# Norm chains in halves at four layer boundaries, and work moved off VectorE in a two-block transformer kernel

## What is computed

```python
def rms_norm(x, g):
    y = x * rsqrt(mean(x * x, axis=-1) + EPS)
    return y * g
for layer in range(2):                      # first block
    a = rms_norm(h, g[layer, 0])
    m = mla_mixer(a) if layer == 0 else hgrn2_mixer(a)
    h = h + rms_norm(m, g[layer, 1])        # post-norm
    a = rms_norm(h, g[layer, 2])
    h = h + rms_norm(relu(a @ w1)**2 @ w2, g[layer, 3])   # post-norm
# second block: rms_norm, dsa_mixer (top-k of indexer scores, then attention), conv FFN,
# rms_norm, retention_mixer, conv FFN
```

## Time and profile before

| | |
|---|---|
| median of 3 runs | 2640.44 us (2637.19 to 2641.26) |
| profiled execution | 2637.47 us, span 2635.7 us |
| PE busy | 2568.2 us, 97% |
| POOL busy | 1938.6 us, 74% |
| DVE busy | 1104.4 us, 42% |
| ACT busy | 662.3 us, 25% |
| HBM traffic | 85 GB/s mean |

### The profile page before, as it was taken

The page is one execution under the profiler, slowest core; times in us unless marked ns, Lnnn a source line. Parts: engine busy times, 40 slices in busy tenths (PEclk is TensorE's granted clock), DMA queues, the critical chain, the costliest instruction groups (busy, mean ns, idle before and its releaser), DMA issues.

```text
span 2635.7 us, 32594 instructions
## 1 busy us (share of the span) xinstructions
PE 2568.2 (97%) x11823; PEld 2089.6 (79%) x11823; DVE 1104.4 (42%) x1907; ACT 662.3 (25%) x1110; POOL 1938.6 (74%) x1664
## 2 busy tenths in 40 slices
PE   6999999998999899999998999999999999999999
PEld 5777888887888688888776888888877877888887
DVE  6543211126767432112587352525442332643433
ACT  2443111014444311001355221203112022321111
POOL 5455988886666588888580888887967856888784
PEclk8999999999999999999998999999999999999999
DMA  5122323332222222332210233332212212333231
GB/s 155 53 72 64 96 96 95 96 97 79 65 77 67 64 96 96 96 95 88 72 65 17 80 96 96 96 98 95 96 64 95 80 64 80 96 96 104 88 108 68
DMA packets 287877, 224.26 MB, mean 85 GB/s; under 512 B 13491, under 2 KB 281756, under 8 KB 287644
## 3 DMA queue, kind: packets, MB, share of 16 engines
q1 hardware_dynamic: 287196, 222.44, 27.5%
q10 hardware_dynamic: 576, 0.40, 0.1%
HBM read 220.72 MB, written 2.10 MB: 85 GB/s over the span
## 4 chain that ended last, share of the span: by engine, by line
PE 90%; DVE 5%; issue 1%; DVEq 1%; ACT 1%; DMA 0%; POOL 0%; ACTq 0%
PE proj L617 26%; PE proj L619 26%; PE proj L618 26%; PE aux L2218 1%; DVE top L1768 1%; DVEq L1771 1%; PE proj L642 1%; PE proj L647 1%; PE proj L643 1%; PE aux L2022 1%; PE aux L2192 1%; PE aux L853 1%; PE proj L795 1%; PE aux L465 0%; PE proj L1961 0%
## 5 line engine op out<-in xcount | busy, mean ns | idle before, releaser
L617 PE MATMUL proj<-a_hi,w_hi 128*128 128x512 f32 x1992 | 795.1, 399 | 0.0
L619 PE MATMUL proj<-a_hi,w_lo 128*128 128x512 f32 x1992 | 776.6, 390 | 0.0
L618 PE MATMUL proj<-a_lo,w_hi 128*128 128x512 f32 x1992 | 775.9, 389 | 0.0
L1245 POOL TENSOR_TENSOR w_hi<-raw,small 128x512 fp32r<-128x512 f32 x373 | 392.9, 1053 | 442.5 <-PE proj L619 343.6
L1252 POOL TENSOR_TENSOR w_hi<-raw,small 128x512 fp32r<-128x512 f32 (+2 forms) x449 | 486.1, 1083 | 187.5 <-PE proj L619 187.3
L1257 POOL TENSOR_TENSOR w_lo<-raw,w_hi 128x512 fp32r<-128x512 f32 (+2 forms) x449 | 592.4, 1319 | 6.0
L1256 POOL TENSOR_TENSOR w_lo<-raw,w_hi 128x512 fp32r<-128x512 f32 x372 | 483.9, 1301 | 29.1
L617 PE MATMUL proj<-g_hi,w_hi 128*128 128x512 f32 x1200 | 470.0, 392 | 0.9 <-POOL w_lo L1257 0.5
L619 PE MATMUL proj<-g_hi,w_lo 128*128 128x512 f32 x1200 | 467.0, 389 | 0.0
L618 PE MATMUL proj<-g_lo,w_hi 128*128 128x512 f32 x1200 | 466.9, 389 | 0.0
L617 PEld LDWEIGHTS proj<-a_hi,w_hi 128*128 128x128 f32 x1992 | 374.5, 188 | 82.8 <-issue 5.3
(11 more groups left out here) (289 smaller groups left out, 2301.9 us busy)
## 6 DMA issues: line engine op xcount, KB each, us to landing
raw<-in_mlp_w SPq DMA_DIRECT2D x64, 1024.0 KB, 5.3
raw<-in_f_w_up SPq DMA_DIRECT2D x88, 512.0 KB, 4.6
raw<-in_b_w_in SPq DMA_DIRECT2D x24, 1024.0 KB, 5.2
raw<-in_hgrn_w_in SPq DMA_DIRECT2D x32, 512.0 KB, 4.9
raw<-in_f_w_down SPq DMA_DIRECT2D x16, 1024.0 KB, 4.9
raw<-in_b_w_out SPq DMA_DIRECT2D x8, 1024.0 KB, 5.1
raw<-in_f_w_down SPq DMA_DIRECT2D x8, 768.0 KB, 4.3
raw<-in_a_w_in SPq DMA_DIRECT2D x5, 1024.0 KB, 5.2
```

Of the source, the lines that this page charges most:

```text
L617: pe.matmul(psum[r][:], w_hi[r][:, w], xh, start=k == 0, stop=False)
L618: pe.matmul(psum[r][:], w_hi[r][:, w], xl, start=False, stop=False)
L619: last = pe.matmul(psum[r][:], w_lo[r][:, w], xh, start=False, stop=k == kc - 1)
L1245: first = pool.tensor_tensor(hi[:, 0:n], src[:, 0:n], nothing.to_broadcast([P, n, P]), ALU.subtract)
```

## The change

Four parts.

1. **Post-norm in two halves of 256 tokens**, at the four boundaries. The sums of the two halves go to two banks, `aux[0]` and `aux[3]`; the last square, the last matmul with ones, Ln, Exp, the multiplication and addition of tile 0 and its `a_hi` are each done per half. ACT's order is Ln 0, Exp 0, Ln 1, Exp 1; the next stage's first matmul still waits for both halves. After an MLP the last `acc` addition is halved too, and the sum of squares of tile 6 comes ahead of it. After an output projection the copy of the last bank goes from ACT to DVE.
2. **Products of ones.** `keep_running` puts matmuls of the ones matrix with itself (128 columns, into an unused bank) into PE's stream: 2 ahead of the half sums (MLPs only), 9 after them (all four).
3. **Start.** The range reduction of the angles, its sines and the sign go behind `take_c(1)`; ACT reloads the logarithm and exponential table after the sines. The tables are loaded one slab later than the small rows.
4. **Selections.** `r_square` and `r_col` are scaled on ACT; the key tile is made by ACT (gain) and POOL (root); both `q_refine` move to POOL, after the splits of query unit 7 and of output unit 2; the indexer's last projection is taken before the key tile is made, and its sum of squares comes before the first score.

```diff
+            def square_half(self, act, src, s):
+                if s == 0:
+                    act.wait_ge(sq_used.sem, self.base + self.chunks - 1 - len(self.tiles))
+                act.activation(self.last[:, HALVES[s]], src[:, HALVES[s]], ACT.Square).then_inc(sq_ready.sem, 1)
...
+                for bank, h in zip(self.banks, HALVES):
+                    last = pe.matmul(bank[:, h], ones[:], self.total[:, h], start=True, stop=False)
+            def sum_half(self, pe, s):
+                h = HALVES[s]
+                pe.wait_ge(sq_ready.sem, self.base + self.chunks + s)
+                pe.matmul(self.banks[s][:, h], ones[:], self.last[:, h], start=False, stop=True).then_inc(sq_used.sem, 1)
+            def root(self, act):
...
+                for s, h in enumerate(HALVES):
+                    act.wait_ge(sq_used.sem, self.base + self.chunks + s)
+                    act.activation(log_ms[:, h], self.banks[s][:, h], ACT.Ln, bias=eps,
+                                   scale=1.0 / self.size).then_inc(logs[s][0], 1)
+                    act.wait_ge(*logs[s])
+                    act.activation(rstd[:, h], log_ms[:, h], ACT.Exp, scale=-0.5).then_inc(roots[s], 1)
...
+        def keep_running(pe, n):
+            for _ in range(n):
+                pe.matmul(aux[2][:, 0:P], ones[:], ones[:], start=True, stop=True)
...
             def dve(self, dve, then=None):
-                dve.wait_ge(*self.norm.ready())
-                for c in range(DC + 1):
+                for s, h in enumerate(HALVES):
+                    scaled, added = (self.scaled, self.added) if s else (self.half_scaled, self.half_added)
+                    dve.wait_ge(*self.norm.half_ready(s))
+                    dve.scalar_tensor_tensor(tmp[0][:, h], tile(acc, 0)[:, h], gain("norm", self.gain_at), rstd[:, h],
+                                             ALU.mult, ALU.mult).then_inc(scaled.sem, 1)
+                    dve.wait_ge(*scaled.at(0))
+                    dve.tensor_tensor(tile(hT, 0)[:, h], tile(hT, 0)[:, h], tmp[0][:, h], ALU.add).then_inc(added.sem, 1)
+                for c in range(1, DC + 1):
...
                 turns_from(pe, self.st.turns, block)
                 self.post.norm.sum(pe)
+                keep_running(pe, 2)
+                for s in range(2):
+                    self.post.norm.sum_half(pe, s)
+                keep_running(pe, 9)
...
+                bank = arrived(act, self.st, DC - 1)
+                for s in range(2):
+                    self.post.norm.square_half(act, bank, s)
...
+                dve.tensor_copy(tile(acc, DC - 1), psum[self.st.bank(DC - 1)][:]).then_inc(*taken(self.st, DC - 1))
...
                         if st.slab_base + q == 2:
-                            small_loads()
+                            row_parts()
+                        if st.slab_base + q == 3:
+                            late_tables()
...
+            def key_scaled():
+                pool.wait_ge(*key_gained.at(0))
+                pool.wait_ge(*n_key.ready())
+                pool.tensor_tensor(dsa_kT, dsa_kT, rstd, ALU.mult).then_inc(key_ready.sem, 1)
...
+                            if st is st_dsa and j == Q0 + 4:
+                                key_scaled()
+                            if st is st_dsa and j == Q0 + DSA_HEADS - 1:
+                                q_refine(0)
+                            if st is st_dsa_o and j == RING - 2:
+                                q_refine(1)
...
-            sine(0, rope_sin, reduced)
-            sine(1, rope_cos, reduced_cos)
             act.wait_ge(norms_ready, 1)
             pre_mla.act(act, h_ready.at, mla_factor)
...
             square_c(1)
+            sine(0, rope_sin, reduced)
+            sine(1, rope_cos, reduced_cos)
+            log_and_exp(act)
...
-            dve.wait_ge(*r_ready.at(2))
-            dve.tensor_scalar(r_square[:], r_square[:], 1.0 / DSA_LAT, None, ALU.mult).then_inc(r_factors.sem, 1)
...
-                    if b == TB - 1 and n == rounds - 2:
-                        q_refine(0)
...
-                if b == 1:
-                    dve.wait_ge(*n_key.ready())
-                    dve.scalar_tensor_tensor(dsa_kT, dsa_cT, qk_gain[:], rstd, ALU.mult, ALU.mult).then_inc(key_ready.sem, 1)
```

More of the change, by code:

```diff
@@ L228, in program @@
         inv_freq, rope_sign, eps = (tab["small"][:, k:k + 1] for k in range(3))
-        zero, halves = tab["small"][:, 3:4], tab["small"][:, 4:6]
+        zero, halves, three = tab["small"][:, 3:4], tab["small"][:, 4:6], tab["small"][:, 6:7]
         lb = sb("lb", 8 * DC)
@@ L493, in ready @@
                 return rstd_ready.sem, i * self.gper + self.gbase + g + 1
+        HALVES = (slice(0, T // 2), slice(T // 2, T))
+        half_log, half_rstd = (shared(f"half_{k}", turns=4) for k in ("log", "rstd"))
         class AddedNorm(Norm):
@@ L531, in program, with __init__ @@
         class LastDirect(AddedNorm):
+            made = 0
+            def __init__(self, chunks, total, load=False):
+                super().__init__(chunks, total, load=load)
+                Norm.squares += 1
+                self.made = LastDirect.made
+                LastDirect.made += 1
+                self.last, self.banks = self.tiles[(chunks - 1) % len(self.tiles)], (self.bank, aux[3])
+            def square_half(self, act, src, s):
+                if s == 0:
+                    act.wait_ge(sq_used.sem, self.base + self.chunks - 1 - len(self.tiles))
+                act.activation(self.last[:, HALVES[s]], src[:, HALVES[s]], ACT.Square).then_inc(sq_ready.sem, 1)
             def add(self, dve, c):
@@ L547, in sum, with half_ready @@
                 pe.wait_ge(sq_used.sem, self.base + self.chunks - 2)
[L548 to L551, removed]
+                for bank, h in zip(self.banks, HALVES):
+                    last = pe.matmul(bank[:, h], ones[:], self.total[:, h], start=True, stop=False)
+                last.then_inc(sq_used.sem, 1)
+            def sum_half(self, pe, s):
[3 more added lines that the diff above has]
+            def root(self, act):
+                if self.gbase > 0:
+                    act.wait_ge(rstd_ready.sem, self.gbase)
+                logs = (half_log.at(self.made), (log_ready.sem, self.gbase + 1))
+                roots = (half_rstd.sem, rstd_ready.sem)
+                for s, h in enumerate(HALVES):
[4 more added lines that the diff above has]
+                    act.activation(rstd[:, h], log_ms[:, h], ACT.Exp, scale=-0.5).then_inc(roots[s], 1)
+            def half_ready(self, s):
+                return self.ready() if s else half_rstd.at(self.made)
         class PairedNorm(Norm):
@@ L918, in act @@
                 turns(act, self.st.turns, block)
-                for c in range(DC):
+                for c in range(DC - 1):
                     emptied(act, self.st, DC + c, self.st.turns - 1)
                     self.post.norm.square(act, tile(acc, c), c)
+                act.wait_ge(*self.half_taken.at(0))
+                self.post.norm.square_half(act, tile(acc, DC - 1), 0)
+                emptied(act, self.st, 2 * DC - 1, self.st.turns - 1)
+                self.post.norm.square_half(act, tile(acc, DC - 1), 1)
                 self.post.norm.root(act)
@@ L978, in pe @@
                 self.post.norm.sum(pe)
+                for s in range(2):
+                    self.post.norm.sum_half(pe, s)
+                keep_running(pe, 9)
             def act(self, act):
-                for m in range(DC):
+                for m in range(DC - 1):
                     bank = arrived(act, self.st, m)
```

122 lines of the change are left out of this document (71 added, 51 removed).

## The result

The changed kernel takes 2624.23 us (median of 5, 2622.59 to 2627.60), the kernel before beside it 2639.40: ratio 0.9947, 95% interval 0.9936 to 0.9957. Its profiled execution is one of 2622.59 with a span of 2620.6, 15.1 shorter than that of before. The forecast of 2625.3 is 1.1 us off. Later runs will show that one of its three terms, the boundaries, came out near its number by chance in this one execution.

What follows compares the result with a forecast made beforehand. PE was taken as the bound, busy 97% of the 2635.7 us span. Start 6.8, boundaries 3.0 and selections 5.3 sum to 15.1 us off 2640.4, giving 2625.3 us; range over the cases 2612 to 2634, the sum's own 2619 to 2631.

Steps and rivals of the forecast that it cites:

- Start, 6.8 us: Kernel start: first matmul at 21.9 instead of 28.76 us, less 0.1 booked against it; gain 6.8 us.
- nearly filled: Between take_c(1) and PE's need of the squares, some 15 us: moved work fills nearly all; 0.1 us booked, 1.5 far bound.
- Boundaries, the arithmetic: Restarts after the four post-norms, from halved chains: 0.1 us later, 0.55 earlier, 0.5 later, 0.5 earlier.
- the alternation with GpSimd: At the boundaries, DVE and POOL operations alternate one for one; a half operation costs a whole POOL operation plus 0.28 us.
- Boundaries, the clock: Four post-norm boundaries: gains of 7.7 us with the clock up, about 0.2 with it down; 3.0 us booked.
- everything fits: Rival: clock stays up at three or four boundaries and DVE slips between POOL's operations; 25 us, 2616; chance 0.20.
- Selections, 5.3 us: Sparse attention: net 3.2 us from DVE's chain, 1.2 and 0.5 between its halves, 0.4 from reordering; sum 5.3 us.
- the meeting with GpSimd: Sparse attention: POOL's later splits slow DVE's normalizations and the selection's last step; 1.6 us lost.
- the reordering: Ahead of the first score: one PE wait goes, another comes, DVE's sum may end earlier; +0.4 us.
- One part gives nothing: Rival: one of start, boundaries or selections yields no gain; 8 us in all, 2632; chance 0.14.

Runs made afterwards that it cites:

- no products: Changed kernel without any products of ones, the post-norm chains still in halves: 2625.78 us.
- the kernel with the boundaries undone: Changed kernel with the four post-norm chains whole again and no products of ones, start and selections kept: 2624.57 us, and 2624.95 when run again.
- more products and GpSimd held: Changed kernel with 12 products (22 at the third boundary) and GpSimd's two w_lo operations held until DVE's last a_lo tile: 2618.23 us, ratio 0.9918.

## Why the prediction came out right, point by point

- *Start, 6.8 us.* Right: first matmul at 21.87 for 21.9, shift 7.7 and 7.5 in the changed kernel, 7.2 in the mean of twelve. What lies above is the clock, which I hadn't counted: from the first matmul to the eighth the shift grows from 6.9 to 7.6. The "nearly filled" 15 us were filled to the last: nothing lost in the changed kernel, 0.64 once the start came 1.4 earlier still.
- *Boundaries, the arithmetic.* Right within 0.1 at all four restarts (no products), and the alternation with GpSimd is shown by holding GpSimd back: 1.37 becomes 0.43. The Trainium skill (SBUF — State Buffer, "Who interferes with whom") has the port pair that the two engines share as an exclusive lock; these rows agree.
- *Boundaries, the clock.* The gains with the clock up were right within 0.2 (1.3, 2.0, 0.9, 2.9). The chances were a third, a half, nothing and a half; in the five traces with nine products the clock was up at boundaries 1 to 4 in four, two, none and four, 2.0 a trace for my 1.3. What failed is that the term had one more step: next in line at the second and fourth boundary is the sum of squares at L533, 1.9 us of the 7.7. And 3.0 us of mean gain (2.7 by its own parts: 0.4, 1.4, -1.0 and 1.9) was booked as if it were certain, while its scatter, and that of the low stretches elsewhere, is as large. In the median the term is 0 +/- 1.5. The reason given for "everything fits" was a reading that misleads: the clock was indeed at 1.00 while PE waited at the shorter stops, but in the same trace it fell at 1300.8 us, 4.4 us behind a stop of 0.45 and with none since. So shorter stops are no safeguard.
- *Selections, 5.3 us.* 6.2 without a further low stretch, 4.7 with one. The 4.8 off DVE's chain were 5.1 at the first wait (it is 2.51, where I had said near 4); the meeting with GpSimd was oversized, 0.6 for 1.6 (the shift falls from 11.5 to 10.9 over the first half); the second half gave 2.1 for 1.7; the reordering -0.2 for +0.4.
- *The sum.* 7.2 + 6.2 + 0 is 13.4, and the kernel with the boundaries undone shows 12.9 and 12.6 in its traces. The medians give more, 13.9 to 15.2 for the changed kernel and 14.4 and 14.8 for that one, since the profiled execution of before lay 1.9 below its median and these did not. So my 15.1 had 0.4 and 0.9 too little at the start and in the attention and 3.0 too much at the boundaries, and the odd low position of the execution it was taken from filled the gap. The range and the sign stood on the first two terms, which are shown; that the number came within 1.1 us and not within 3 is luck.
- *Rivals.* "Everything fits" (2616) did not come with nine products; with more products and GpSimd held, its 25 us came to within 4. "One part gives nothing" is what the medians say of the boundaries, at some 2625 and not 2632, since the other two gave more; I had meant by it the start or the attention. Alone, these two gave 6.6 and 6.3 us of median, 12.9 together.

## What to carry to other kernels

Cover nearly all of a stop of PE or leave it: nine products that cover 2 of 5 us buy a draw in a lottery, eighteen, which left 0.6 to 2.2 us, bought 3.6 us and a spread of 0.2 in four of five executions. Splitting a chain into halves gave 0.1 us here while GpSimd took turns with it and the clock was down, so first look who shares its operands' memory and whether that work has slack. Before crediting a part of some 2 us, look at what the same stretch does in a second execution and what untouched stretches do in the same one.

## What the runs showed of the hardware

- The granted clock fell to 0.50 after stops as short as 0.78 us (HGRN2's end, seven of the fourteen traces) and 0.98 us (the sparse attention's key root, L478 in the changed kernel, five of them), and not in the others. It also fell with no stop at all, behind 3 us of products of 128 and 32 columns (661.0 us in the kernel with the selections alone, and the same place in one of the two with the boundaries undone). Why it falls in some executions and not in others was not found; the phase of the gate's own watch would explain it but cannot be seen here.
- In the sparse attention the selections gave 6.2 us in the four traces without products of ones and 4.7 in seven of the eight with them, which have one low stretch more, or a longer one: in four behind the stop of 0.98 us at L478, in three near 1290 us, where the longest stop is 0.45. The eighth, the changed kernel's first, has the one at L478 and missed the other. The stops are the same in all. Whether the products bring it or the phase does is open.
- In the one execution profiled of each kernel, eighteen products of ones of 128 columns (4.18 us together) went with the clock up at all four restarts, where PE still stood 0.6 to 2.2 us behind them; so did twelve and twenty-two, with 0.5 to 1.4 us. Sixteen did not at the third boundary: the clock fell after PE had stood 2.12 us, where it had stayed up after 2.23 with eighteen.
